# Two transformer blocks in one program: the opening's loads, transposes and table inputs put in another order

## The chip, the core and the metric

The kernel runs on one core of a Trainium2 chip: TensorE (PE), VectorE (DVE), ScalarE (ACT), GpSimd (POOL) and SyncE (SP), each with an instruction stream of its own, tied together by semaphores, and 16 DMA engines that move data between DRAM and the on-chip memory SBUF. TensorE writes into eight banks of PSUM. The metric is the device time of one execution in microseconds (us), the median over several; less is better.

## The reference

Two blocks over 256 tokens of 2048 features in float32. Only the head of the first block lies at the places of the change; in the first of its two layers it is, for x and for the context ctx alike:

```python
def first_block(x, c, ctx, c_ctx, ada_w, ada_b, norm_g, w_in, ...):
    for l in range(DEPTH):
        shift, scale, gate = jnp.split(jax.nn.silu(c) @ ada_w[l] + ada_b[l], 3, axis=-1)
        shift_c, scale_c, gate_c = jnp.split(jax.nn.silu(c_ctx) @ ada_w[l] + ada_b[l], 3, axis=-1)
        h = rmsnorm(x, norm_g[l]) * (1.0 + scale[:, None]) + shift[:, None]
        hc = rmsnorm(xc, norm_g[l]) * (1.0 + scale_c) + shift_c
        ...
        qc, kc, vc, upc, ufc, gc = split_proj(hc @ w_in[l])
        kc = rmsnorm(kc.reshape(B, C, N_KV_HEADS, HEAD_DIM), k_norm_g[l])
        q, k, v, up, uf, g = split_proj(h @ w_in[l])
        q = apply_axial_rope(rmsnorm(q..., q_norm_g[l]), cos, sin)
        k = apply_axial_rope(rmsnorm(k..., k_norm_g[l]), cos, sin)
        ...   # attention, pooling, Fourier mixing, gates, w_out, residual
    return rmsnorm(x, final_norm_g)
```

## The kernel before

**Chunks.** Every weight matrix is cut into chunks of 512 KB (`Chunk`), in a list `chunks` in the order in which TensorE multiplies them. A chunk of `ada_w` (an ada chunk) is multiplied as it is, by the silu of c and c_ctx: two float32 products in column groups of one bank (line 1221). A chunk of `w_in` and the others is split first: ScalarE rounds it to a high part (line 1463), VectorE subtracts that from it for a low part (line 1694), and TensorE does three fast products for each pair of tiles (lines 1240 to 1242: high x high, high x low, low x high), 24 products of 512 columns for a k/v chunk.

**Buffers.** SyncE loads the chunks in the order of the list `queue`, which before the change is equal to `chunks`, into `NRAW` = 8 buffers RAW. Load i waits until chunk i - 8 has been multiplied (an ada chunk; semaphore `chunk_multiplied`) or until its low part is made (any other; `split_lo`); SyncE issues in order, so one load that waits holds all behind it. The `NSPL` = 4 buffers SPL hold the split parts. `run_ahead` writes the split of a chunk into the engines' order `START_AHEAD` = 3 places ahead of the chunk that is being multiplied (from place 72 on 5).

**The order of the side work.** All engines take their instructions from one list `order`, into which `run_chunks` writes the products chunk by chunk, and between them tasks from the list `hi`. `pop_side(n)` takes n tasks from it. In the opening an ada chunk takes 2 tasks at every second chunk, a k/v chunk one for each half. So where a task stands in `hi` decides where it stands in the order of each engine, and an engine does what stands there strictly in order.

**The opening.** `start(u)` for u = 0 to 3 lays out two ada groups of 8 chunks, the scale (4 + u) and the shift (u) of features 512u to 512u + 511, and with u > 0 two k/v chunks among them; the last two follow. In places of `chunks`: ada 0 to 27, k/v at 28, 33, 46, 51, 64, 69, 70 and 71. Meanwhile:

- `square_x`, ScalarE: the squares of x and ctx.
- `turn_x(j)`, j = 0 to 15: TensorE turns 128 features of all tokens (line 1283), VectorE copies them out into XT (line 1705). Banks 0 to 2 take turns.
- `first_rstd`, after the 16 columns: `rstd_a` on VectorE and GpSimd (mean, power, four diagonals; lines 1711, 2102, 1716) and `rstd_b` on TensorE (line 1290), which spreads 1/rms over a bank.
- `tile_h(0, k, s)`: h of feature tile k for source s in three steps, VectorE, ScalarE, VectorE (lines 1738, 1481, 1743). Each needs the rms rows and the ada columns of its group, which come over `ada_out`, `ada_turn` (lines 1473, 1297, 1724).
- after the last shift group: `spill`, GpSimd's DMAs of XT to DRAM (4.19 MB, line 2097), since XT's place is used for the rows of q, k, v; `load_tables`, ScalarE's queue, three DMAs with the rope factors and the norm gains (lines 1490 to 1492), into one of the four TMP buffers; `tables`, VectorE (lines 1754, 1757); `load_dft`, GpSimd's queue, which waits for the second half of the copy.

`kv_out` follows the last k/v chunk: it flushes `hi`, then the k rows are copied out of banks 0 and 2 by ScalarE (line 1499) and of 1 and 3 by VectorE (line 1765), then the v columns of all four banks by ScalarE (line 1505). The first q chunk writes the same banks. From there on (`main0[1]`: q, pool, Fourier, gates) `mixed` puts two ada chunks, of the list `left`, behind every two others.

## Time and profile before

| | us |
|---|---|
| median of three runs | 2414.23 |
| lowest and highest | 2413.69, 2423.34 |
| the profiled execution | 2421.02 |
| its span, first to last instruction | 2419.2 |
| granted TensorE clock, mean | 0.984 |

The profile's page gives for each engine its busy time, for 40 equal slices (60.5 us each) the busy share in tenths, and the chain of work that ended last. A timeline row reads: start, length, engine, line, operation, output and input, how often, and in brackets the idle time before it and what ended it. "PEclk" is the granted share of TensorE's full clock of 2.4 GHz. A DMA share of 1.05 is what full engines show here.

### The profile page before, as it was taken

The page shows a single profiled execution, that of the slowest core. Times are in us where ns is not written, and L with a number is a line of the kernel's source. Part 1 is how long each engine was busy: PE and PEld are TensorE (multiplying, and loading weights), DVE is VectorE, ACT ScalarE, POOL GpSimd, SP SyncE. Part 2 cuts the span into 40 slices and gives each one's busy share as a digit, 9 for nine tenths or more (in the row PEclk, how much of TensorE's full clock was granted, in tenths as well). Part 3 has the DMA queues.
Part 4 walks back from the last instruction along what each step waited for, and adds up shares of the span by engine and source line. Part 5 has one row for each costly group of instructions (what it writes and reads, how often), then busy time and mean ns, then how long its engine had stood idle before and what let it go on. Part 6 is the DMA issues. An engine that isn't in the chain of part 4 may idle for free.

```text
span 2419.2 us, 30889 instructions
## 1 busy us (share of the span) xinstructions
PE 2316.2 (96%) x12239; PEld 1862.5 (77%) x12239; DVE 1313.2 (54%) x2114; ACT 1045.0 (43%) x1599; POOL 249.1 (10%) x325
## 2 busy tenths in 40 slices
PE   5889999999999979999999988999999999999998
PEld 2467777677777857678888867888888888888887
DVE  2444533132323254445777875667765777567764
ACT  2332333332322154445555654555544555355543
POOL 1000100000001121100011124111100110001111
PEclk9999999999999989999999998999999999999998
DMA  9864343335655456734566553566655555555552
GB/s 368 298 243 166 127 146 110 119 127 174 215 171 173 155 198 209 263 104 132 185 196 185 184 166 122 170 189 189 192 184 184 190 187 183 189 185 184 189 187 83
DMA packets 347023, 436.68 MB, mean 181 GB/s; under 512 B 13848, under 2 KB 269280, under 8 KB 345984
## 3 DMA queue, kind: packets, MB, share of 16 engines
q1 hardware_dynamic: 341376, 413.19, 51.6%
q0 software_dynamic: 3408, 16.38, 1.9%
q10 hardware_dynamic: 2096, 5.15, 0.6%
q8 instruction: 97, 1.59, 0.3%
q14 instruction: 46, 0.38, 0.0%
HBM read 428.37 MB, written 6.29 MB: 180 GB/s over the span
## 4 chain that ended last, share of the span: by engine, by line
PE 84%; DVE 6%; ACT 4%; DMA 3%; issue 2%; POOL 1%; SPq 0%; ACTq 0%; POOLq 0%; DVEq 0%
PE ps L1265 31%; PE ps L1266 16%; PE ps L1260 5%; PE ps L1262 5%; PE ps L1261 5%; PE ps L1240 4%; PE ps L1242 4%; PE ps L1241 4%; PE ps L1221 3%; DVE SPL L1694 2%; DMA RAW<-in_w_in_dram 2%; ACT SPL L1463 2%; PE ps L1312 1%; PE ps L1329 1%; PE ps L1355 1%
## 5 line engine op out<-in xcount | busy, mean ns | idle before, releaser
L1265 PE MATMUL ps<-HS,SPL 128*128 128x512 f32 x3456 | 1226.4, 400 | 5.9 <-POOL HS L2166 3.9
L1694 DVE TENSOR_TENSOR SPL<-RAW,SPL 128x1024 fp32r<-128x1024 f32 x592 | 750.5, 1271 | 634.2 <-ACT SPL L1463 631.7
L1266 PE MATMUL ps<-HS,SPL 128*128 128x256 f32 x3456 | 969.0, 280 | 0.0
L1463 ACT ACTIVATE SPL<-RAW 128x1024 fp32r<-128x1024 f32 x592 | 622.0, 1055 | 476.4 <-PE ps L1266 308.2
L1265 PEld LDWEIGHTS ps<-HS,SPL 128*128 128x128 f32 x3456 | 652.9, 189 | 166.4 <-POOL HS L2166 3.5
L1266 PEld LDWEIGHTS ps<-HS,SPL 128*128 128x128 f32 x3456 | 655.4, 190 | 2.0 <-issue 1.9
L1240 PE MATMUL ps<-SPL,HS 128*128 128x512 f32 x576 | 248.6, 432 | 27.2 <-ACT XT L1505 8.2
L1242 PE MATMUL ps<-SPL,HS 128*128 128x512 f32 x576 | 228.7, 397 | 0.0
L1241 PE MATMUL ps<-SPL,HS 128*128 128x512 f32 x576 | 228.3, 396 | 0.0
L1260 PE MATMUL ps<-HS,SPL 128*128 128x512 f32 x480 | 199.5, 416 | 1.2 <-DVE HS L1850 1.2
L1262 PE MATMUL ps<-HS,SPL 128*128 128x512 f32 x480 | 187.9, 391 | 0.0
L1261 PE MATMUL ps<-HS,SPL 128*128 128x512 f32 x480 | 187.8, 391 | 0.0
L1240 PEld LDWEIGHTS ps<-SPL,HS 128*128 128x128 f32 x576 | 110.8, 192 | 75.5 <-issue 18.5
L1241 PEld LDWEIGHTS ps<-SPL,HS 128*128 128x128 f32 x576 | 111.1, 193 | 26.9 <-issue 6.0
L1242 PEld LDWEIGHTS ps<-SPL,HS 128*128 128x128 f32 x576 | 110.3, 192 | 24.9
L2161 POOL TENSOR_TENSOR MM<-MM,GX 128x256 f32<-128x256 f32 x96 | 60.5, 650 | 653.7 <-DVE MM L1831 653.7
L1221 PE MATMUL ps<-RAW,CW 128*32 128x512 f32 x768 | 115.8, 637 | 9.7 <-DMA RAW<-in_ada_w_dram 7.8
L1260 PEld LDWEIGHTS ps<-HS,SPL 128*128 128x128 f32 x480 | 90.6, 189 | 41.0 <-issue 15.3
L1597 ACT ACTIVATE TMP<-XT 128x256 f32<-128x256 f32 (+1 forms) x74 | 33.9, 458 | 182.4 <-DVE XT L1862 113.7
L2154 POOL TENSOR_TENSOR TMP<-TMP 128x256 f32<-128x256 f32 (+1 forms) x67 | 60.7, 906 | 484.4 <-ACT TMP L1597 481.8
L1261 PEld LDWEIGHTS ps<-HS,SPL 128*128 128x128 f32 x480 | 90.5, 189 | 21.3 <-issue 3.8
L1262 PEld LDWEIGHTS ps<-HS,SPL 128*128 128x128 f32 x480 | 90.5, 189 | 19.7
(271 smaller groups left out, 1717.7 us busy)
## 6 DMA issues: line engine op xcount, KB each, us to landing
RAW<-in_w_in_dram SPq DMA_DIRECT2D x208, 512.0 KB, 5.7
RAW<-in_ada_w_dram SPq DMA_DIRECT2D x192, 512.0 KB, 4.8
RAW<-in_ffn_w_up_dram SPq DMA_DIRECT2D x192, 512.0 KB, 3.6
RAW<-in_w_out_dram SPq DMA_DIRECT2D x96, 512.0 KB, 4.5
RAW<-in_ffn_w_down_dram SPq DMA_DIRECT2D x96, 512.0 KB, 3.3
x_spill<-XT POOLq DMA_DIRECT2D x2, 2048.0 KB, 14.5
XT<-x_spill POOLq DMA_DIRECT2D x1, 4096.0 KB, 15.9
MM<-in_x_dram ACTq DMA_DIRECT2D x2, 1024.0 KB, 11.2
```

What stands on the lines that cost most here:

```text
L1221: m = mm(PS[6][32 * q:32 * q + 32, :], CW[:, 2 * k:2 * k + 32], raw_of(i)[:, kk * 512:(kk + 1) * 512], start=kc < 2, stop=kc >= 6, skip_gr ...
L1240: mm(PS[b][:, :], hr, wr, start=k == 0, stop=False, skip_group_check=True)
L1241: mm(PS[b][:, :], hr, wl, start=False, stop=False, skip_group_check=True)
L1242: m = mm(PS[b][:, :], hl, wr, start=False, stop=k == KT - 1, skip_group_check=True)
L1260: mm(PS[b][:, :], wr, hr, start=k == 0, stop=False, skip_group_check=True)
L1261: mm(PS[b][:, :], wr, hl, start=False, stop=False, skip_group_check=True)
L1262: m = mm(PS[b][:, :], wl, hr, start=False, stop=k == KT - 1, skip_group_check=True)
L1265: mm(PS[b][:, :], wr, hh, start=k == 0, stop=False, skip_group_check=True)
L1266: m = mm(PS[b][:, 256:512], wl, hh[:, 0:256], start=False, stop=k == KT - 1, skip_group_check=True)
L1463: act(SPL[:, (n - 1) % NSPL, 0, :], raw_of(i), ACT.Copy).then_inc(s_hi, 1)
L1694: tt(w[:, 1, :], raw_of(s["i"]), w[:, 0, :].bitcast(F32), ALU.subtract).then_inc(s_lo, 1)
L2154: tt(acc, acc, T(s["slot"])[:, 0:s["nt"] * 128], ALU.add).then_inc(s_accp, 1)
```

## The change

Eight edits, all at the opening:

- the k/v chunks stand after 8 of the 16 chunks of a `start` and at its end: places 24, 33, 42, 51, 60, 69, 70, 71
- `queue` is no longer `chunks`: each k/v chunk of the opening is loaded `KV_EARLY` = 3 places before its place of use. `c.load` is a chunk's place among the loads, `c.pos` among the products; the waits of both sides are written with the two
- in `start(0)` each ada chunk takes 2 tasks (side 3), so that two columns of x are turned per chunk; 12 idle tasks instead of 6 keep the first one where it was
- `first_rstd` becomes two tasks, after columns 1 and 3
- `spill` stands right behind the last column
- `tables_in` of the first layer as well, in a place of MM that holds x until it is turned, instead of in a TMP buffer; `tables` is put behind `load_dft`
- 4 ada chunks of `left` stand between the last k/v chunk and the first q chunk
- splits run 3 places ahead before place 71, 7 before place 76, 5 behind

```diff
         def load_ahead():
             while at["loaded"] < len(queue):
-                i = at["loaded"] - NRAW
                 last = []
-                if i >= 0 and queue[i].shape:
-                    if i >= at["taken"]:
+                if at["loaded"] >= NRAW:
+                    c = queue[at["loaded"] - NRAW]
+                    if c.pos >= (at["taken"] if c.shape else at["pos"]):
                         return
...
+                    last = [(s_lo, split_no[c.pos]) if c.shape else (s_chunk, c.pos + 1)]
...
-            while at["taken"] < min(len(queue), at["pos"] + (START_AHEAD if at["pos"] < 72 else at["ahead"])):
+            while at["taken"] < min(len(chunks), at["pos"] + (START_AHEAD if at["pos"] < 71 else 7 if at["pos"] < 76 else at["ahead"])):
...
-                    pop_side(2 if c.group.side == 2 and c.kc % 2 == 0 else 0)
+                    pop_side(2 if c.group.side == 3 or c.group.side == 2 and c.kc % 2 == 0 else 0)
...
-                x["tab"], last = take()
-                put("tables_in", l=l, slot=x["tab"], last=last + ([(s_colT, 3)] if both else x["ended"]))
+                if not both:
+                    x["tab"], last = take()
+                    put("tables_in", l=l, tab=T(x["tab"]), last=last + x["ended"])
...
-                cs = ada_group(0, 4 + u, 2) + ada_group(0, u, 2)
+                side = 2 if u else 3
+                cs = ada_group(0, 4 + u, side) + ada_group(0, u, side)
...
-                    if u == 3:
-                        put("spill", last=[multiplied()])
                     hi.extend(staged([tile_h(0, k, s, x, h) for k in range(4 * u, 4 * u + 4) for s in range(2)])
-                              + ([load_tables, tables, load_dft] if u == 3 else []))
+                              + ([load_tables, load_dft, tables] if u == 3 else []))
...
-                return cs[:12] + kv[2 * u - 2:2 * u - 1] + cs[12:] + kv[2 * u - 1:2 * u] if u else cs
+                return cs[:8] + kv[2 * u - 2:2 * u - 1] + cs[8:] + kv[2 * u - 1:2 * u] if u else cs
...
-        lay_out(main0[0] + mixed(main0[1], left))
+        n_start = len(main0[0])
+        head = main0[0] + left[:4]
+        del left[:4]
+        lay_out(head + mixed(main0[1], left))
...
+        for i in range(n_start):
+            if queue[i].shape:
+                queue.insert(i - KV_EARLY, queue.pop(i))
...
-        hi.extend([turn_x(j) for j in range(KT)] + [first_rstd])
+        turns = [turn_x(j) for j in range(KT)]
+        hi.extend(turns[:2] + [first_rstd_a] + turns[2:4] + [first_rstd_b] + turns[4:] + [lambda: put("spill", last=[]),
+                     lambda: put("tables_in", l=0, tab=MM[:, 7680:8192], last=[(s_turn, KT), (s_colT, 3)])])
```

What it moves, engine by engine. SyncE, the first loads; before:

```order
L1188 DMA RAW<-in_ada_w_dram 128x2x512 x8
L1188 DMA RAW<-in_ada_w_dram 128x2x512 [waits chunk_multiplied] x20
L1188 DMA RAW<-in_w_in_dram 128x2x512 [waits chunk_multiplied]
L1188 DMA RAW<-in_ada_w_dram 128x2x512 [waits chunk_multiplied] x4
L1188 DMA RAW<-in_w_in_dram 128x2x512 [waits chunk_multiplied]
L1188 DMA RAW<-in_ada_w_dram 128x2x512 [waits chunk_multiplied] x2
L1188 DMA RAW<-in_ada_w_dram 128x2x512 [waits split_lo]
L1188 DMA RAW<-in_ada_w_dram 128x2x512 [waits chunk_multiplied] x4
L1188 DMA RAW<-in_ada_w_dram 128x2x512 [waits split_lo]
```

and with the change:

```order
L1199 DMA RAW<-in_ada_w_dram 128x2x512 x8
L1199 DMA RAW<-in_ada_w_dram 128x2x512 [waits chunk_multiplied] x13
L1199 DMA RAW<-in_w_in_dram 128x2x512 [waits chunk_multiplied]
L1199 DMA RAW<-in_ada_w_dram 128x2x512 [waits chunk_multiplied] x7
L1199 DMA RAW<-in_ada_w_dram 128x2x512 [waits split_lo]
L1199 DMA RAW<-in_w_in_dram 128x2x512 [waits chunk_multiplied]
L1199 DMA RAW<-in_ada_w_dram 128x2x512 [waits chunk_multiplied] x7
L1199 DMA RAW<-in_ada_w_dram 128x2x512 [waits split_lo]
```

The first k/v load (`in_w_in`) goes from the 29th place to the 22nd, and the first load that waits for a split from the 37th to the 30th.

VectorE, from the second column of x on: before, the last columns, the first split and the rms chain (the columns before are left out; line 1694 is the split, 1705 the copy of a column, 1711 and 1716 the rms chain, 1738 the first step of h):

```order
L1694 TENSOR_TENSOR SPL<-RAW,SPL 128x1024 [waits split_hi]
L1705 COPY XT<-ps 128x2x256 [waits x_turned]
L1711 TENSOR_SCALAR SM<-SM 128x4 [waits x_squares]
L1716 TENSOR_SCALAR TMP<-IDN,SM 128x128 [waits rows_turned,rms_power]
L1716 TENSOR_SCALAR TMP<-IDN,SM 128x128 x3
L1738 SCALAR_TENSOR_TENSOR TMP<-XT,S,ps 128x256 [waits ada_turned,ada_scale,rstd_rows]
L1738 SCALAR_TENSOR_TENSOR TMP<-XT,S,ps 128x256 [waits ada_turned]
```

and with the change, the same work (lines 1705, 1716, 1722 and 1727, 1749):

```order
L1716 COPY XT<-ps 128x2x256 [waits x_turned] x2
L1722 TENSOR_SCALAR SM<-SM 128x4 [waits x_squares]
L1727 TENSOR_SCALAR TMP<-IDN,SM 128x128 [waits rms_power]
L1727 TENSOR_SCALAR TMP<-IDN,SM 128x128 x3
...
L1716 COPY XT<-ps 128x2x256 [waits x_turned] x14
L1735 TENSOR_REDUCE ADA<-ps 128x8 [waits ada_turned]
L1739 TENSOR_TENSOR ADA<-ADA,VV 128x8 [waits ada_summed]
L1749 SCALAR_TENSOR_TENSOR TMP<-XT,S,ps 128x256 [waits rows_turned,ada_scale,rstd_rows]
L1749 SCALAR_TENSOR_TENSOR TMP<-XT,S,ps 128x256 [waits ada_turned]
L1705 TENSOR_TENSOR SPL<-RAW,SPL 128x1024 [waits split_hi]
```

The rms chain stands between the second and the third column, all columns stand ahead of the first split.

TensorE, from the last k/v product to the first q product; before (1242 is the last k/v, 1240 the first q):

```order
L1240 MATMUL ps<-SPL,HS 128x512
L1241 MATMUL ps<-SPL,HS 128x512
L1242 MATMUL ps<-SPL,HS 128x512
L1240 MATMUL ps<-SPL,HS 128x512 [waits v_out,split_lo]
L1241 MATMUL ps<-SPL,HS 128x512
```

and with the change:

```order
L1252 MATMUL ps<-SPL,HS 128x512
L1253 MATMUL ps<-SPL,HS 128x512
L1232 MATMUL ps<-RAW,CW 32x512 [waits raw0_in,ada_out]
L1232 MATMUL ps<-RAW,CW 32x512
L1232 MATMUL ps<-RAW,CW 32x512 [waits raw1_in]
L1232 MATMUL ps<-RAW,CW 32x512
L1232 MATMUL ps<-RAW,CW 32x512 [waits raw2_in]
L1232 MATMUL ps<-RAW,CW 32x512
L1232 MATMUL ps<-RAW,CW 32x512 [waits raw3_in]
L1232 MATMUL ps<-RAW,CW 32x512
L1251 MATMUL ps<-SPL,HS 128x512 [waits v_out,split_lo]
L1252 MATMUL ps<-SPL,HS 128x512
```

Four ada chunks (line 1232) stand where TensorE went straight into the wait for the v copies.

## Rows read from the trace of the kernel before

**Rows 1.** The page, its parts 1 and 2: TensorE and the DMA engines over 40 slices
```profile
PE   5889999999999979999999988999999999999998
...
DMA  9864343335655456734566553566655555555552
```

**Rows 2.** Busy time by stretch: start:end, length, each engine, PEclk, DMA share, GB/s
```profile
0.00:4.00 4.00, 0.00 (x0) 0.00 (x0) 0.19 (x2) 0.00 (x0) 2.95 (x10) 1.00 0.48 119
...
4.00:60.00 56.00, 35.45 (x187) 13.33 (x187) 14.57 (x33) 12.37 (x14) 6.37 (x13) 0.99 1.05 386
...
60.00:84.00 24.00, 21.02 (x116) 12.59 (x116) 14.25 (x37) 8.92 (x17) 0.62 (x1) 0.89 0.58 203
...
100.00:112.00 12.00, 11.45 (x76) 6.13 (x68) 7.08 (x18) 4.56 (x10) 0.00 (x0) 1.00 0.88 304
...
134.00:148.00 14.00, 12.17 (x53) 9.43 (x52) 8.09 (x18) 4.80 (x9) 0.00 (x0) 1.00 1.01 413
...
156.70:161.00 4.30, 4.27 (x10) 3.43 (x11) 2.64 (x6) 2.27 (x4) 0.72 (x1) 0.50 0.07 27
...
161.00:200.00 39.00, 39.00 (x185) 29.38 (x185) 14.11 (x25) 8.28 (x12) 2.99 (x3) 1.00 0.38 131
```

**Rows 3.** Chain that ended last, 0 to 200 us: start, length in us, what
```profile
47.35 9.06 DMA RAW<-in_w_in_dram
...
61.67 2.06 PE ps L1290 x8
...
110.73 7.36 DMA RAW<-in_w_in_dram
...
157.92 0.43 PE ps L1242
...
165.09 0.24 PE ps L1242
```

**Rows 4.** Timeline while x is turned, and SyncE's next issue after the hole
```profile
36.52 1.09 PE L1283 MATMUL ps<-IDN,MM 128*128 128x128 f32 x8
...
37.21 1.29 DVE L1705 COPY XT<-ps 128x512 f32<-128x512 f32 x2 [0.73 <-PE ps L1283]
...
65.59 18.18 SPq L1188 DMA_DIRECT2D RAW<-in_ada_w_dram  x12
```

**Rows 5.** Waits of SyncE's queue, 0 to 200 us: total, times, longest
```profile
SPq L1188 <- DVE SPL L1694: 13.6, 7, 6.6
```

**Rows 6.** Timeline from the last k/v product to the first q product
```profile
148.88 0.66 ACT L1499 ACTIVATE XT<-ps 128x256 f32<-128x256 f32 x2 [6.19 <-PE ps L1242]
...
153.33 0.43 DVE L1754 TENSOR_TENSOR XT<-TMP,GX 128x256 f32<-128x256 f32 x1 [10.13 <-DMA GX<-in_k_norm_g_dram]
...
155.54 0.94 ACT L1505 ACTIVATE XT<-ps 128x256 f32<-128x256 f32 x3 [5.73 <-DVE XT L1765]
...
156.73 0.77 PE L1240 MATMUL ps<-SPL,HS 128*128 128x512 f32 x1 [7.89 <-ACT XT L1505]
```

**Rows 7.** DMA issues of the page: count, KB each, median us to landing
```profile
x_spill<-XT POOLq DMA_DIRECT2D x2, 2048.0 KB, 14.5
```

**Rows 8.** Timeline around the fifth to the eighth k/v chunk
```profile
120.47 0.80 PE L1240 MATMUL ps<-SPL,HS 128*128 128x512 f32 x1 [2.65 <-DVE SPL L1694]
...
127.51 1.92 PE L1221 MATMUL ps<-RAW,CW 128*32 128x512 f32 x16
...
130.06 1.18 POOL L2097 DMA_DIRECT2D x_spill<-XT  x2 [69.44 <-PE ps L1221]
...
133.17 1.22 DVE L1694 TENSOR_TENSOR SPL<-RAW,SPL 128x1024 fp32r<-128x1024 f32 x1
...
136.78 0.47 PE L1240 MATMUL ps<-SPL,HS 128*128 128x512 f32 x1 [1.18 <-DVE HS L1743]
...
148.40 0.75 POOL L2117 DMA_DIRECT2D XT<-in_k_dft_dram  x1 [17.16 <-DMA x_spill<-XT]
```

More of the change, by code:

```diff
@@ L20 @@
 AHEAD = 5
+KV_EARLY = 3
 START_AHEAD = 3
@@ L285, in run_ahead @@
                     last = [(s_chunk, chunk_split[at["split"] - NSPL] + 1)] if at["split"] > NSPL else []
-                    put("split", i=i, last=last)
+                    put("split", i=chunks[i].load, last=last)
                 at["taken"] += 1
@@ L1056, in two_block_program @@
         count["columns"] = 1
-        hi.extend([lambda: put("square_x")] + [idle] * 6 + [lambda: (columns([0, 1, 3, 4], False), columns([5, 6], True))])
+        hi.extend([lambda: put("square_x")] + [idle] * 12 + [lambda: (columns([0, 1, 3, 4], False), columns([5, 6], True))])
         def turn_x(j):
```

34 lines of the change are left out of this document (17 added, 17 removed).

## The prediction

> **What bounds the kernel now.** I read the page first. TensorE's line stands at nines almost throughout, but the first slices hold a five and an eight while the DMA engines stand at 9, 8, 6 there [rows 1]. So one stretch works by another limit. The busy time by stretch shows it: from 4 to 60 us the 16 DMA engines are full (share 1.05, 386 GB/s), from 60 to 84 us they fall to 0.58, from 100 to 112 to 0.88, and from 161 us on TensorE is full and the DMA engines idle more than half [rows 2]. Everything edited lies ahead of 161 us, so the question is how much earlier the same TensorE work of the first layer starts.
>
> Two holes stand there. The first is in the loads. The first k/v chunk is issued at 47.35 us and lands 9.06 us later; its split holds VectorE and ScalarE, behind which stands the last copy of x and the rms chain, and TensorE multiplies the rms rows only at 61.67 [rows 3]. TensorE consumes no weights meanwhile, no RAW buffer comes free, and SyncE issues no ada load until 65.59 [rows 4]. SyncE also waits 13.6 us in seven waits for the low half of a split [rows 5]. In engine time: 60 to 84 us lose (1.05 - 0.58) / 1.05 x 24 = 10.7 us, 100 to 112 lose (1.05 - 0.88) / 1.05 x 12 = 1.9, the shallow stretches between a further 0.2: 12.8 us lost before the fifth k/v chunk (the 65th load, chunk 64) lands at 110.73 + 7.36 = 118.1 [rows 2, 3]. As a control: 65 loads of 524 KB, 4.2 MB of x and ctx and some 0.6 of small inputs at 386 GB/s are 100.7 us; with 2.8 us lost in the first four (119 GB/s there [rows 2]) and the 12.8 they give 116.3, and it landed 1.8 later, the way from the last byte to the semaphore. The opening is bound by DMA traffic plus these holes.
>
> The second hole is at the end of k/v. ScalarE copies banks 0 and 2 at 148.88, but the rope tables wait for their inputs until 153.33, because VectorE has them ahead of its copies of banks 1 and 3; the v copies go at 155.54 and TensorE starts the q columns at 156.73, after 7.89 us idle [rows 6], which puts the end of k/v at 148.84.
>
> **The loads and the copy of x.** After the change the last ada chunk of the opening (chunk 68) is load 71, since the three last k/v chunks stand ahead of it. I go by landing times, from 118.1 us:
> - the 12.8 us of lost engine time go, as the k/v loads are there before their turn and the rms chain runs between turned columns long before the first k/v split: -12.8
> - the copy of x to DRAM, two DMAs of 2 MB [rows 7], ran from 130.06 with loads no one was yet waiting for, and now runs inside the full stretch. 4.19 MB at the 413 GB/s that 134 to 148 us show with both kinds mixed [rows 2] are 10.2 us: +10.2. Its lower bound is 0 (if it fell wholly into holes), its upper 18.3, from its issue at 130.06 until GpSimd's wait for it ends at 148.40 [rows 8]; I take the mixed rate, since no row shows a load stand still for it
> - the rope inputs, 0.39 MB in small pieces: +1.0 (0.5 to 2)
> - seven more loads before chunk 68, at 0.524 MB / 386 GB/s = 1.36: +9.5
> - turning x at twice the rate. Two turned columns take TensorE 1.09, and VectorE copies them in 1.29 [rows 4]; an ada chunk is a quarter of 1.92 [rows 8]. One chunk and two columns are so 1.6 us, longer than the 1.36 of a load; ten such places with the rms product and two ada turns let TensorE fall behind the loads from about chunk 10, by 2.3 us at chunk 15: +2.3 (0 to 6; below nothing it can't be, the loads are at full rate there now)
>
> Sum: 128.3, and with 0.5 to multiply the chunk 128.8, against 127.51 + 1.92 = 129.4 before [rows 8]. So the holes filled pay for the copy, and little more: -0.6 us. The Trainium skill (DMA: Bandwidth & Descriptors, section Issuing engines are not separate DMA queues) says that DMAs of all issuing engines run on the same 16 DMA engines and interleave. By that rule the copy is paid wherever the engines are full, as I take it; without it the result below would be 10.2 us better. The trace agrees: share 1.01 with both kinds in flight [rows 2].
>
> **The last three k/v chunks.** From chunk 68 to the last product were 148.84 - 129.4 = 19.4 us: three chunks of some 5.5, plus waits for h. One split of 1.22 us stood between the ada column and the scaled x on VectorE (133.17) [rows 8]; the order now has three splits ahead of the ada column and none behind: -1.2, which is just the 1.18 that TensorE waits there. Against it stands the clock: ahead of these three TensorE has five or six single ada chunks, each when its load lands. Before, the chunk after such a stretch began at 120.47 with products of 0.80, after a wait of 2.65 [rows 8], and lost some 1.8 us. The wait is gone now, since the split is early, so I take half: +0.9 (0 to 1.8). The Trainium skill (TensorE: Matmul & The Clock Gate, What's actually happening) holds that the slow clock is the default and activity lifts it; by it thin work too may bring the slow clock, which would be the 1.8. From 4 to 60 us such work stood at 0.99 [rows 2]; the trace decides neither.
>
> So k/v ends at 128.8 + 19.4 - 1.2 + 0.9 = 147.9, against 148.84: -0.9.
>
> **The end of k/v.** With tables made and the copy done, there remain the copies out of the banks: ScalarE two (0.66) and four v copies (0.94 for three), with TensorE starting 0.25 behind them [rows 6]: 2.2 us. TensorE does four ada chunks in it, 1.92 us [rows 8], taken from later in the layer, where TensorE is full. Before 7.89, now 2.2: -5.7, and -1.9 for the four chunks. The clock, 0.50 from 156.7 to 161 [rows 2], holds ten products at 0.43 instead of 0.24 [rows 3]: -1.9 with the gap gone. Their splits are made while k/v runs (the table of places ahead is 7 there), so they add nothing.
>
> **The rest.** The ada groups end four chunks earlier in the later stages; the same steps fall at other places. No row here shows what that moves; the nearest is the wait for h of 1.18 us [rows 8], so I put 0 with two such waits on either side, -2.4 to +2.4.
>
> Sum: -0.9 - 5.7 - 1.9 - 1.9 = -10.4 us. The profiled execution took 2421.0 (span 2419.2), 6.8 over the median of the three runs, 2414.2; the opening it shows belongs to either. So 2421.0 - 10.4 = 2410.6 for such an execution, and 2414.2 - 10.4 = 2403.8 for the median: 2404.
>
> **Rivals.**
> *The copy and the turning cost less.* If the copy starts at about 48 us, where the doubled turning leaves the loads thin, it uses just those 2.3 us; with the clock kept (-0.9), half the rope price, and the second layer gaining 1.5, it is -10.4 - 2.3 - 0.9 - 0.5 - 1.5 = -15.6: 2398.6. For it: loads and copy interleave. Against: by 48 us the thin stretch is nearly over.
> *The copy costs what it took.* The copy displaces loads for its 18.3 us, or the turning costs its upper 6 and the rope inputs and clock theirs (+5.6): +6 to +8, so about -3: 2411. For it: the DMA of x out and the weights lie in one set of engines, and it took 14.5 us a piece [rows 7]. The Trainium skill (DMA: Bandwidth & Descriptors, Queues, rings and completion order) says that an engine takes turns between queues packet by packet. By it loads may be thinned while the copy runs, and made up behind it: no change to the sum, only an idle TensorE then.
> *TensorE becomes the bound at the slow clock (the other side).* While the copy thins the loads, TensorE idles, and its clock falls. A k/v chunk at 0.43 a product takes 24 x 0.43 = 10.3 us, eight ada chunks at twice 0.48 take 7.7, with turns some 19.4 us, against 12.2 for nine loads. If the clock stayed low over four such rounds, each costs 7.2: +29, so +18.4: 2433. It decides only if 24 products in a row don't bring the clock back; before, they did within ten (156.7 to 161) [rows 2]. That speaks strongly against it.
> *The change doesn't do what it says.* If the rms chain still waited for a split, the hole at 54 to 65 would stay, with the copy on top: +12.8 - 10.4 = +2.4: 2416.6. The order of VectorE shows the chain ahead of every split, so hardly.
>
> **How the numbers follow.** Forecast -10.4: 0.52. Copy and turning cheap: 0.27. Copy at its full time: 0.13. No effect of the order: 0.04. Slow clock: 0.04. The 80% range reaches to the cheap case with the spread of the before runs (3 below) and to the dear one: 2395 to 2413. A measurement of this kernel can tell 0.5% from no change, 12.1 us. The forecast's own spread of about 4 us puts a third of it past 12.1 (0.17), and the cheap case nearly all (0.25): faster 0.42; slower by over 12.1 only the slow clock, 0.04; the rest, 0.54, within.
>
> **What the profile after would show.** Right: DMA share about 1.05 without a hole from 4 to 125 us but for a shallow dip near 40 to 50; the copy issued near 48; the last ada chunk near 129; k/v ending near 148; TensorE going on with ada chunks and the q columns 2 us behind, at clock 1.00. Wrong: a hole in the loads after 50 us (a split still stops SyncE), k/v chunks that start at half clock one after another, or the last k/v product after 152.

## The result, and the profile after

| | median us | range | runs |
|---|---|---|---|
| before | 2414.6 | 2413.7 to 2423.3 | 4 |
| after | 2442.2 | 2441.8 to 2445.3 | 4 |
| ratio after / before | 1.0105 | 95% interval 1.0081 to 1.0129 | |
| forecast | 2404 | 2395 to 2413 | |

The change makes the kernel slower by 1.05% in the ratio (the medians are 27.6 us apart), where a gain of 10 us was forecast; the worst rival stood at 2433. The profiled execution took 2442.5 (span 2440.7), so it is typical; that of before was 6.4 over the median of the four runs.

First the stretches of the opening, in the columns of [rows 2] (start:end, length, busy time of TensorE, its weight loads, VectorE, ScalarE and GpSimd, granted clock, DMA share, GB/s):

```profile
36.00:56.00 20.00, 19.30 (x124) 9.13 (x120) 11.53 (x22) 2.45 (x4) 1.18 (x2) 1.00 0.75 238
56.00:72.00 16.00, 3.78 (x8) 0.33 (x8) 2.76 (x7) 0.58 (x2) 0.00 (x0) 0.57 0.99 405
72.00:84.00 12.00, 11.32 (x52) 7.58 (x54) 5.00 (x12) 3.90 (x7) 0.00 (x0) 0.72 0.65 233
84.00:100.00 16.00, 13.55 (x76) 6.16 (x66) 7.50 (x18) 4.88 (x9) 0.00 (x0) 1.00 1.01 369
100.00:125.00 25.00, 22.89 (x119) 11.66 (x116) 9.12 (x23) 6.80 (x12) 0.00 (x0) 1.00 1.02 365
```

Where the engines moved 386 GB/s from 4 to 60 us before [rows 2], they now move 238 from 36 to 56, while TensorE is busy 19.3 of 20 us. The hole of 60 to 84 us is not gone but has moved to 72 to 84, and the shallow 100 to 112 is filled. TensorE's timeline (start, length, line, operands, count, idle time before and what ended it) shows both causes:

```profile
42.29 1.05 PE L1232 MATMUL ps<-RAW,CW 128*32 128x512 f32 x4
43.27 1.09 PE L1294 MATMUL ps<-IDN,MM 128*128 128x128 f32 x8
44.30 1.05 PE L1232 MATMUL ps<-RAW,CW 128*32 128x512 f32 x4
...
51.30 0.66 PE L1294 MATMUL ps<-IDN,MM 128*128 128x128 f32 x4
...
58.21 1.86 PE L1232 MATMUL ps<-RAW,CW 128*32 128x512 f32 x4 [2.72 <-DMA RAW<-in_ada_w_dram]
69.96 1.92 PE L1232 MATMUL ps<-RAW,CW 128*32 128x512 f32 x4 [9.89 <-DMA RAW<-in_ada_w_dram]
...
73.41 0.78 PE L1251 MATMUL ps<-SPL,HS 128*128 128x512 f32 x1
```

A place with one ada chunk and two turned columns takes 2.0 us, from 42.29 to 44.30. The last column is turned at 51.3, and GpSimd issues the copy of x at 52.98. After that TensorE gets no ada chunk between 58.2 and 70.0: it idles 9.89 us, and starts the first k/v chunk at half clock (0.78 for the first product).

The last ada chunk of the opening ends at 142.0 (forecast 128.8), the last k/v product at 161.0 (forecast 147.9). The end of k/v is then as forecast, and right behind it comes something that wasn't:

```profile
161.00 1.93 PE L1232 MATMUL ps<-RAW,CW 128*32 128x512 f32 x16
...
172.51 0.66 PE L1315 MATMUL ps<-IDN,XT 128*128 128x128 f32 x2 [3.66 <-DVE XT L1806]
172.82 0.78 PE L1251 MATMUL ps<-SPL,HS 128*128 128x512 f32 x1
173.39 0.63 PE L1252 MATMUL ps<-SPL,HS 128*128 128x512 f32 x1
```

The four ada chunks take 1.93, the first q product starts at 163.12, 2.1 us behind k/v and at full clock (granted clock 1.00 from 161 to 165 us, where it was 0.50 before [rows 2]). But TensorE then waits 3.66 us for a norm that it has to turn (the k rows, normed by VectorE; L1315 is L1304 of before) and loses the clock: its products have a length of 0.63 instead of 0.39. What VectorE waited for itself stands in the rows of ScalarE, SyncE and VectorE:

```profile
162.09 0.88 SPq L1199 DMA_DIRECT2D RAW<-in_w_in_dram  x2
...
165.59 1.06 ACT L1474 ACTIVATE SPL<-RAW 128x1024 fp32r<-128x1024 f32 x1 [2.72 <-DMA RAW<-in_w_in_dram]
...
166.68 2.56 DVE L1705 TENSOR_TENSOR SPL<-RAW,SPL 128x1024 fp32r<-128x1024 f32 x2 [4.82 <-ACT SPL L1474]
```

Two q loads, the ninth and the tenth from the first early ada chunk on, take the buffers of the first early chunks and are issued only at 162.09, when these have been multiplied. Their splits stand ahead of the norm on ScalarE and VectorE, so the norm waits for two loads.

The largest part lies further on. The waits of TensorE from 165 to 1100 us, of before first and of after below it (line, what it waited for: total, times, longest):

```profile
PE ps L1240 <- POOL HS L2111: 5.5, 4, 3.6
PE ps L1304 <- DVE MM L1795: 4.5, 2, 3.8
...
PE ps L1240 <- ACT MM L1499: 2.9, 1, 2.9
PE ps L1297 <- ACT TMP L1473: 2.6, 3, 1.0
...
PE ps L1304 <- DVE XT L1798: 0.8, 2, 0.4
```

```profile
PE ps L1315 <- DVE MM L1806: 12.5, 3, 6.5
PE ps L1315 <- DVE XT L1806: 10.0, 5, 3.7
PE ps L1308 <- ACT TMP L1484: 6.8, 3, 3.9
PE ps L1251 <- POOL HS L2122: 4.0, 4, 1.4
```

TensorE waited 5.3 us for the norms of q and its neighbours (L1304) in this stretch, and now 22.5 (L1315, the same line); for the ada column (L1297, now L1308) 2.6 and now 6.8.

### The profile page after: what moved, and what is told of

The parts are those of the page before. It is cut to its first block, busy times and chain, and to the rows that moved or that the text cites. A ratio compares the mean times of both kernels' runs of the same rounds, so it can differ in the third digit from the quotient of the medians.

```text
span 2440.7 us, 30874 instructions
## 1 busy us (share of the span) xinstructions
PE 2319.6 (95%) x12239; PEld 1858.3 (76%) x12239; DVE 1315.7 (54%) x2114; ACT 1044.1 (43%) x1599; POOL 250.4 (10%) x325
## 4 chain that ended last, share of the span: by engine, by line
PE 84%; DVE 6%; ACT 4%; DMA 3%; issue 2%; POOL 1%; SPq 0%; ACTq 0%; POOLq 0%; DVEq 0%
PE ps L1276 31%; PE ps L1277 15%; PE ps L1271 5%; PE ps L1273 4%; PE ps L1272 4%; PE ps L1251 4%; PE ps L1253 4%; PE ps L1252 4%; PE ps L1232 3%; DMA RAW<-in_ada_w_dram 2%; DVE SPL L1705 2%; ACT SPL L1474 2%; PE ps L1323 1%; PE ps L1340 1%; PE ps L1366 1%
## 5 line engine op out<-in xcount | busy, mean ns | idle before, releaser
L1232 PE MATMUL ps<-RAW,CW 128*32 128x512 f32 x768 | 123.3, 631 | 29.8 <-DMA RAW<-in_ada_w_dram 27.9
L1271 PEld LDWEIGHTS ps<-HS,SPL 128*128 128x128 f32 x480 | 90.1, 188 | 42.6 <-issue 16.1
```

The source lines that it names most:

```text
L1232: m = mm(PS[6][32 * q:32 * q + 32, :], CW[:, 2 * k:2 * k + 32], raw_of(c.load)[:, kk * 512:(kk + 1) * 512], start=kc < 2, stop=kc >= 6, sk ...
L1271: mm(PS[b][:, :], wr, hr, start=k == 0, stop=False, skip_group_check=True)
```

## The experiments

Each kernel's ratio is to the kernel before on the same chip, with its 95% interval. "First q product" is where the opening ends in the profiled execution (156.73 before; before_delay4, which has the code of the kernel before up to there, shows 160.09, so a single profile of the opening is good for some 3 us). "Growth" is how much later the same products of TensorE run than in the kernel before at 1040 to 1080 us, less what it was at 160 to 200 us: the n-th start of each line of code (ada products left out) is compared in both traces, and the median of the differences taken. Kernels that leave the order behind the opening as it was (before_copy_early, before_rms_early) show -2.0 and -3.2, so a growth within some 3 us of nothing is none. A growth without a subtraction is the difference alone.

| kernel | ratio | interval | first q product | growth, us |
|---|---|---|---|---|
| after | 1.0105 | 1.0081 to 1.0129 | 163.12 | 27.1 - 10.6 = 16.5 |
| copy_late | 1.0108 | 1.0089 to 1.0128 | 161.96 | 26.4 - 7.3 = 19.1 |
| turn_old | 1.0086 | 1.0066 to 1.0105 | 152.16 | 16.2 - 0.1 = 16.1 |
| no_head | 1.0012 | 0.9999 to 1.0026 | 160.76 | -0.7 - 2.7 = -3.4 |
| before_head | 1.0099 | 1.0073 to 1.0124 | 163.21 | 24.6 - 7.0 = 17.6 |
| head_phase | 1.0008 | 0.9994 to 1.0023 | 161.46 | 0.5 - 3.5 = -3.0 |
| before_delay4 | 1.0086 | 1.0059 to 1.0112 | 160.09 | 19.2 - 3.7 = 15.5 |
| before_head8 | 1.0025 | 1.0007 to 1.0043 | 162.17 | 6.3 - 5.9 = 0.4 |
| nh_turn_old | 0.9953 | 0.9935 to 0.9970 | 153.46 | -7.3 + 3.8 = -3.5 |
| nh_to_copy_late | 0.9956 | 0.9936 to 0.9975 | 149.07 | -2.7 |
| copy_halves | 0.9959 | 0.9947 to 0.9971 | 149.34 | -3.1 |
| kv_late | 1.0005 | 0.9993 to 1.0018 | 163.44 | -3.5 |
| turn_pairs | 1.0007 | 0.9992 to 1.0022 | 162.22 | 0.2 |
| copy_at_kv0 | 1.0008 | 0.9992 to 1.0023 | 164.02 | -0.5 |
| pairs_halves | 0.9970 | 0.9951 to 0.9989 | 153.83 | -0.7 |
| before_copy_early | 0.9993 | 0.9974 to 1.0011 | 156.94 | -2.0 |
| before_rms_early | 0.9993 | 0.9978 to 1.0008 | 159.03 | -3.2 |

### The four early ada chunks: taken out, and alone

```diff
 (after)
-        head = main0[0] + left[:4]
-        del left[:4]
+        head = main0[0]
-... (START_AHEAD if at["pos"] < 71 else 7 if at["pos"] < 76 else at["ahead"])
+... (START_AHEAD if at["pos"] < 72 else at["ahead"])
```

> The changed kernel without the four ada chunks between the k/v and the q columns (they go back to their places later in the layer), and with the k/v table of places ahead (3, then 5) of the kernel before. The opening up to the last k/v product stays as in the changed kernel. Theory A (the later losses come from these four chunks: the two q loads that wait for them, the seven splits made ahead that stand in front of the k norm chain, and every later ada group at another place): the wait of 3.66 us of TensorE for the turned norms and the half clock from 172 us go, and the offset to the kernel before stays at some 11 to 13 us from 170 us to the end instead of growing to 27 and ending at 22. Time 2442 - 7 = 2435. Theory B (the four chunks fill a gap of 2 us and the later growth has another cause): 2442 + 2 = 2444, with the same growth after 250 us.

Measured: 1.0012. The growth is gone (-3.4), and so is the wait of 3.66 us. Its size had been expected at 7 us; it was some 22 (2442.2 to 2420.0 in the medians, 0.9% in the ratios). Theory A holds with three times its price. The edit also takes back the table of seven places, so the chunks alone are the next run.

```diff
 (before)
-        lay_out(main0[0] + mixed(main0[1], left))
+        head = main0[0] + left[:4]
+        del left[:4]
+        lay_out(head + mixed(main0[1], left))
```

> The kernel before with one part of the change alone: four ada chunks of later groups stand between the k/v columns and the q columns. The number of places looked ahead stays at its old values. They fall into the 7.89 us in which TensorE waits for the v copies, so they are free there and give back 1.9 us later. Theory A (moving the ada groups costs in the rest of the layers): 2414 - 2 + 8 = 2420, and the offset against the kernel before grows in the stretch 200 to 1050 us. Theory B (the move is neutral there): 2412.

Measured: 1.0099, nearly the whole loss of the change from four chunks in another place. Its trace has a pair of waits for turned norms near 223 and 229 us (the change has the same 0.90 and 2.26 at 226.54 and 232.18), again near 287 and 293, and larger ones in the second layer, where the kernel before has 3.79 us and none:

```profile
163.21 0.76 PE L1242 MATMUL ps<-SPL,HS 128*128 128x512 f32 x1 [10.13 <-DVE SPL L1696]
222.95 0.63 PE L1306 MATMUL ps<-IDN,XT 128*128 128x128 f32 x4 [0.93 <-DVE XT L1797]
228.59 0.63 PE L1306 MATMUL ps<-IDN,XT 128*128 128x128 f32 x4 [2.26 <-DVE XT L1797]
...
918.55 1.09 PE L1306 MATMUL ps<-IDN,MM 128*128 128x128 f32 x4 [4.50 <-DVE MM L1797]
925.70 1.09 PE L1306 MATMUL ps<-IDN,MM 128*128 128x128 f32 x4 [6.07 <-DVE MM L1797]
```

The first row is another cost, of this kernel alone. Most of its 10.13 us is the wait for the v copies that the kernel before has too (the last ends at 160.87 here). Behind them ScalarE and VectorE make the first q split, since that chunk now stands four places later and wasn't within the places looked ahead while k/v ran: 2.3 us more. The change's table of seven places took that part away (0.20 there).

What differs at 222.95 is seen against the same group in the kernel before:

```profile
208.70 0.47 PE L1240 MATMUL ps<-SPL,HS 128*128 128x512 f32 x1 [0.59 <-DVE XT L1765]
...
211.55 0.60 PE L1297 MATMUL ps<-IDN,TMP 128*128 128x128 f32 x4
...
215.75 0.69 DVE L1795 TENSOR_TENSOR XT<-TMP 128x512 f32<-128x512 f32 x1
...
217.48 0.60 PE L1304 MATMUL ps<-IDN,XT 128*128 128x128 f32 x4
```

The group starts at 208.70, an ada column is turned at 211.55 (12 products in), and the first norm at 217.48 (36 products in), 1.0 us after VectorE has finished it (215.75 + 0.69). With the four chunks elsewhere the group starts at 216.32 and no ada column is due. The steps beside the products stand in one list and are given out one per half chunk, so the norm's turn moves forward by the step that the ada column held: to 222.95, 24 products in. VectorE's chain ends at 222.11 + 0.69, too late: TensorE waits 0.93 for it, and 2.26 for the second norm. The order was traced at this one group; that the larger waits of the second layer come in the same way rests on the next three runs.

### Phase, or chunks done early?

By phase is meant where an ada group of eight chunks ends against the weights group into which it is mixed: at its end, as in the kernel before, or in its middle.

```diff
 (after: the first four places inside the first q group stay bare)
-        lay_out(head + mixed(main0[1], left))
+        lay_out(head + main0[1][:4] + mixed(main0[1][4:], left))
```

> The changed kernel with the four early ada chunks kept between the k/v and the q columns, but taken from the first four places inside the first q group, which then has its first four chunks bare. From the sixth q chunk on every ada chunk stands where it stood in the kernel before. Theory A (phase: an ada group that ends in the middle of a weights group no longer puts its column and turn between the end of a group and the first turned norm, so the norm chain of VectorE comes too late; 0.9 and 2.3 us at each such place): the waits of TensorE for turned norms of 0.9 and 2.3 us near 225 and 290 us, and of 4.5 and 6.5 near 920 go, the offset to the kernel before stays flat from 190 us on. Time 2442 - 16 = 2426. Theory B (any four chunks moved cost in this way, wherever from, by the splits and loads they shift): 2442. The wait of 3.66 us at 172 us and the half clock behind it may stay by both, since the two q loads still wait for the four.

Measured: 1.0008, with the four chunks as early as in the change. Growth -3.0. TensorE's waits from 165 to 1100 us in it:

```profile
PE ps L1251 <- POOL HS L2122: 5.8, 3, 3.5
PE ps L1315 <- DVE MM L1806: 4.2, 2, 3.8
...
PE ps L1315 <- DVE XT L1809: 1.1, 3, 0.4
PE ps L1315 <- DVE XT L1806: 1.1, 2, 0.6
```

The norms are back at 6.4 us. The wait near 172 us, which both theories let stand, went too (0.61 at 167.79). That is no sign against the two q loads: with the four places bare, the third and fourth q chunks are loads 78 and 79, which SyncE had issued by 145.1 and which landed by 151.7, and the splits ahead of the norm are theirs. In the change they were loads 80 and 81, issued at 162.09 and landed at 165.56 and 166.90. So this edit takes away two costs, the wait for two loads and the moved end of the later ada groups; the offset at 160 to 200 us (10.6 and 3.5) has the first, with 1.7 that the opening itself ended earlier, the growth (16.5 and -3.0) the second.

```diff
 (before: the same four places bare, nothing early)
-        lay_out(main0[0] + mixed(main0[1], left))
+        lay_out(main0[0] + main0[1][:4] + mixed(main0[1][4:], left))
```

> The kernel before with one thing changed: the first four places inside the first q group stay bare of ada chunks, so that every ada group from the ninth on ends four chunks LATER than before; none is done early. Theory A (it is the phase, an ada group ending in the middle of a weights group instead of at its end, and not that chunks were taken ahead): the same waits as with four taken ahead, 0.9 and 2.3 us for the turned norms near 215 to 290, some 10 near 920, and 16 to 20 us in all: 2416 + 16 = 2432. Theory B (loads and splits are shifted by the chunks taken ahead): 2416.

Measured: 1.0086, growth 15.5, with waits of 0.92 and 2.26 at 218.47 and 224.11. Four chunks later cost as four chunks earlier.

```diff
 (before)
-        lay_out(main0[0] + mixed(main0[1], left))
+        head = main0[0] + left[:8]
+        del left[:8]
+        lay_out(head + mixed(main0[1], left))
```

> The kernel before with eight ada chunks (one whole group) between the k/v and the q columns, taken from later. Theory A (phase): every later group ends where one ended before, so from 200 us on the offset stays flat; the q columns start later, since their loads wait for the eight (about 10 us idle as with four, and 3.8 us of work that is given back later): 2416 + 5 = 2421. Theory B (each chunk taken ahead costs): more than the 24 us that four cost, 2440 or above.

Measured: 1.0025, growth 0.4. Eight early cost a quarter of what four do, and only in the opening. The three runs agree that the growth hangs on whether an ada group ends where it ended before, at the end of a weights group.

### The opening: turning x, and the copy

```diff
 (after)
-                side = 2 if u else 3
+                side = 2
-... [idle] * 12 ...
+... [idle] * 6 ...
```

> The changed kernel with x turned at the old rate: two columns at every second ada chunk, and six empty steps instead of twelve ahead of them; all else stays. Theory A (a lone ada chunk between turned columns takes TensorE as long as two do, so the doubled turning let TensorE and with it the loads fall behind): the DMA share from 36 to 56 us comes back from 0.75 to about 1.0, some 4 to 6 us of engine time, but the copy of x is issued some 8 us later and starves the loads there just the same. Time 2442 - 4 = 2438, with the end of the opening (last ada chunk) near 138. Theory B (the doubled turning costs the 2.3 us that the forecast gave it): 2440. Theory C: the later copy meets the first k/v chunks and the time rises by 3 to 5.

Measured: 1.0086 against 1.0105, 4.6 us, with intervals that overlap; the offset to the kernel before at 160 us falls from 10.6 to 0.1, more than the time shows. The share from 36 to 56 us is 1.05, as theory A said, and the one from 72 to 84 us 0.98 instead of 0.65.

> The changed kernel without the four early ada chunks and with x turned at the old rate; the early loads of the k/v weights, the early rope inputs, the early copy of x and the early rms chain stay. If the two costs are apart and add up (the four chunks 22 us, the turning 6 to 10 us in the opening), it stands 7 to 10 us under the kernel without the four chunks: 2418 - 6 = 2412, ratio 0.9975, with the last k/v product near 150. If the doubled turning only cost because of the four chunks: 2420.

This kernel has that edit and the one of no_head. Measured: 0.9953, faster than the kernel before by 0.3 to 0.65%, where 0.9975 was expected. Its stretches:

```profile
36.00:56.00 20.00, 16.69 (x118) 8.51 (x116) 11.93 (x25) 2.25 (x3) 0.60 (x1) 1.00 1.05 387
56.00:72.00 16.00, 11.57 (x48) 7.03 (x48) 7.70 (x17) 4.91 (x9) 1.18 (x2) 0.79 1.03 404
72.00:84.00 12.00, 11.15 (x60) 5.92 (x60) 4.48 (x12) 3.88 (x7) 0.00 (x0) 1.00 1.02 362
```

No hole is left up to 125 us. With the turning of the change, everything else equal, it is 1.0012 (no_head): the first q product stands 7.3 us later (160.76 against 153.46), and the ratios differ by 0.6%, 14 us; the trace bears out some 7.

```diff
 (after, behind the last turned column; and in start 3)
-                     [..., lambda: put("spill", last=[]), ...]
+                    if u == 3:
+                        put("spill", last=[multiplied()])
```

> The changed kernel with one thing put back: the copy of x to DRAM is issued at the end of the fourth start (about 130 us) as in the kernel before, no longer behind the last turned column. Theory A (the copy starves the loads): it is what makes TensorE wait 2.72 and 9.89 us for ada loads between 58 and 70 us and run at half clock until 80. Without it the 16 loads land about 10 us earlier, the first k/v chunk runs at full clock, and the last ada chunk of the opening ends near 130 instead of 142; the late copy then makes the rope tables or the v copies wait a little. Time about 2442 - 9 = 2433. Theory B (bytes only count, wherever they move): the last ada chunk comes 10 us earlier as well, but the copy then delays the last k/v chunks and q by as much, so the time stays within 3 us of 2442. Theory C: TensorE's slow turning is what costs, and the time stays at 2442 because the loads are late anyway.

Measured: 1.0108, the same as after. The last ada chunk of the opening ends 8.5 us earlier (133.6), but TensorE then waits 5.28 us for scaled x at 152.52: nearer to theory B.

> As the one before it in this set, and the copy of x at its old place (about 130 us) as well. If the copy starves the loads wherever they are needed at once, the early place costs 10 us of engine time at 57 to 72 us and the late one delays the last three k/v chunks and the tables by some 5: 3 to 5 us less than with the early copy, 2408. If the engines are full from 4 to 140 us in either case and the copy costs its bytes at both places: the same, 2412. If the late copy holds the tables and the scaled x: 2415.

> The kernel with x turned at the old rate and without the four early ada chunks, with the first 2 MB of the copy of x issued behind the last turned column, and the other 2 MB at the end of the fourth start (about 127 us). If the copy costs its bytes wherever the engines are full, and only the part that falls into the thin stretch of 56 to 72 us (share 0.53 where the copy is late, 1.03 where it is early) is free: the best of the three, 2403. If it is all the same: 2406, as with either place of the whole copy.

Measured: 0.9956 and 0.9959. The whole copy early (0.9953), late, or half and half are the same within the intervals. Where it is late, the hole in the loads is back:

```profile
56.00:72.00 16.00, 11.40 (x56) 6.38 (x56) 8.52 (x19) 4.91 (x9) 0.00 (x0) 0.89 0.53 180
...
59.20 0.76 PE L1252 MATMUL ps<-SPL,HS 128*128 128x512 f32 x1 [3.50 <-DVE HS L1755]
```

So the early k/v loads and the early rms chain, which this kernel has, don't remove it: TensorE waits 3.50 us for scaled x and then multiplies the first k/v chunk, no buffer comes free, and the engines stand at 0.27 from 60 to 64 us and at 0.00 from 64 to 68. That is (1.05 - 0.53) / 1.05 x 16 = 7.9 us of engine time, and in nh_turn_old it is the copy that fills it. The profiled first q product is 4.4 us earlier with the late copy (149.07), which the times don't confirm. That the half-and-half version would be best isn't shown.

```diff
 (before: the copy alone)
-                    if u == 3:
-                        put("spill", last=[multiplied()])
-        hi.extend([turn_x(j) for j in range(KT)] + [first_rstd])
+        hi.extend([turn_x(j) for j in range(KT)] + [lambda: put("spill", last=[]), first_rstd])
```

> The kernel before with one part alone: the copy of x to DRAM issued right behind the last turned column (about 54 us) instead of at 130 us. Theory A (it starves the ada loads behind it by 10 to 12 us): part of that falls into the hole that stands there anyway (TensorE waits 7.64 us for the rms chain and the loads stand still until 65.59), so the loads come some 6 us later, and the gain at the end (scaled x and tables no longer wait for the copy) is 3 at most: 2418 + 3 = 2421. Theory B (the copy fits the hole between 56 and 72 us, with a DMA share of 0.63): 2418 - 5 = 2413.

Measured: 0.9993, no difference, though the copy fills the stretch from 56 to 72 us (share 1.03, before 0.63): neither theory's price.

```diff
 (no_head, copy at the seventh ada chunk of start 1, ahead of the first k/v chunk)
+                if u == 1:
+                    cs[6].then = lambda: put("spill", last=[multiplied()])
```

> The changed kernel without the four early ada chunks, x turned at twice the rate as in the change, and the copy of x put eight ada chunks later, just ahead of the first k/v chunk. Theory A (what the early copy costs hangs on what TensorE has in hand while the copy takes the engines: eight ada chunks that each need a load, as in the change, and it idles 10 us; or a k/v chunk of 6 us whose load and split are there): TensorE's idle 9.9 to 10.6 us shrinks to 3 or less, and the time is 2407, as with the old turning. Theory B (the doubled turning itself costs 7 us, since TensorE falls behind the loads at 36 to 50 us): 2415 to 2418, as the kernel without the four chunks.

Measured: 1.0008. TensorE's idle time behind the copy did shrink, to 3.68 us at most (10.57 in no_head), as theory A said, and the time did not move: theory B. The long idle stretch looks dear, but its length doesn't set the time, since the DMA engines are full in it.

```profile
36.00:56.00 20.00, 19.22 (x124) 9.02 (x120) 12.00 (x23) 2.85 (x5) 0.00 (x0) 1.00 0.78 245
56.00:72.00 16.00, 10.78 (x40) 5.79 (x40) 6.07 (x16) 2.91 (x6) 1.18 (x2) 0.79 0.93 361
72.00:84.00 12.00, 7.33 (x26) 1.14 (x28) 1.23 (x1) 1.06 (x1) 0.00 (x0) 0.86 1.02 391
```

Against the three rows of nh_turn_old above, (387 - 245) x 20 = 2.8 MB were not moved in the first and (404 - 361) x 16 = 0.7 MB in the second: 9.1 us at 387 GB/s. The first q product stands 10.6 later.

```diff
 (no_head: four columns behind two ada chunks)
-... pop_side(2 if c.group.side == 3 or c.group.side == 2 and c.kc % 2 == 0 else 0)
+... pop_side((4 if c.group.side == 3 else 2 if c.group.side == 2 else 0) if c.kc % 2 == 0 else 0)
```

> The changed kernel without the four early ada chunks, and with the same doubled turning given out in fours: two ada chunks, then four turned columns, where the change puts two columns behind each chunk. Theory A (a lone ada chunk between turned columns takes TensorE 1.0 us, as much as two in a row): four columns and two chunks take 2.2 + 1.0 = 3.2 us for two loads (2.7 us) instead of 4.0, so most of the shallow stretch at 36 to 56 us goes; from 2420 down by 3 to 5: 2416. Theory B (the columns themselves, their banks and their copies out are what takes the time): four columns in a row wait for VectorE, no gain, 2420 or above. The early copy starves the loads in either case.

Measured: 1.0007 against 1.0012. Two chunks and four columns do take 3.0 us instead of 4.0 (42.31 to 45.33 in its timeline), but no time came back, and 36 to 56 us moved 303 GB/s against the 295 of no_head. The kernels with the change's turning show 238 (after), 245 (copy_at_kv0), 251 (head_phase) and 295 there, so this window alone doesn't tell. Theory A fell as a remedy, and that the lone chunk is the whole of the turning's cost is not shown.

> As the one before it, with the doubled turning given out in fours behind two ada chunks, and only half of the copy ahead of the first k/v chunk, the other half at the end of the fourth start. A candidate: if theory A of the run before holds, the turned columns are done 2 us sooner than in the change and no load is starved for long: 2404, as the best so far (0.9959 of the kernel before). If the doubled turning costs by itself: 2412.

Its edits are those of the last two, with one half of the copy there and the other in start 3. Measured: 0.9970, between; not better than the old turning.

### The early loads and the early rms chain

```diff
 (nh_turn_old)
-KV_EARLY = 3
+KV_EARLY = 0
```

> The kernel with x turned at the old rate and without the four early ada chunks (0.9953 of the kernel before), with the k/v weights loaded in their own places instead of three places ahead. Theory A (the hole at 54 to 65 us came from a k/v split for which the rms chain and the last copy of x waited; both the early loads and the early rms chain are needed): each k/v chunk waits some 2.6 us for its split again, as in the kernel before at 94 and 120 us, 5 to 8 us lost, 2407 + 5 = 2412. Theory B (the early rms chain alone fills the hole, and the loads are bound by bytes, so their order means nothing): 2407.

Measured: 1.0005 against 0.9953, 12 us. Five of the eight k/v chunks wait for their split, 3.60 to 5.55 us, where it was 2.65 before [rows 8]; three of them:

```profile
91.75 0.79 PE L1250 MATMUL ps<-SPL,HS 128*128 128x512 f32 x1 [3.60 <-DVE SPL L1704]
107.97 0.79 PE L1250 MATMUL ps<-SPL,HS 128*128 128x512 f32 x1 [3.79 <-DVE SPL L1704]
123.09 0.80 PE L1250 MATMUL ps<-SPL,HS 128*128 128x512 f32 x1 [3.87 <-DVE SPL L1704]
```

```diff
 (before: the rms chain alone; first_rstd split in two as in the change)
-        hi.extend([turn_x(j) for j in range(KT)] + [first_rstd])
+        hi.extend(turns[:2] + [first_rstd_a] + turns[2:4] + [first_rstd_b] + turns[4:])
```

> The kernel before with one part alone: the rms chain of x goes between the turned columns (its first half behind the second column, its second behind the fourth) instead of behind the last. Theory A (the chain stood behind a split for which it waited): TensorE multiplies the rms rows near 45 us instead of 61.67, VectorE's wait falls away, the DMA share from 60 to 84 us rises from 0.58 to 0.8 or more, and the time falls by 4 to 8: 2418 - 6 = 2412. Theory B (the split itself, waiting for its 9 us landing, is the hole, whatever stands behind it): 2418.

Measured: 0.9993, no difference; the share from 56 to 72 us is 0.61 (before 0.63), and the first k/v chunk waits 6.19 us for scaled x. The time is that of theory B. That the landing of the split's chunk is the hole doesn't follow: with early loads and a late copy the hole is there too (nh_to_copy_late).

## Why the prediction was wrong, and where it was right

**"The rest": the step that failed most.** The forecast put 0 with 2.4 us on either side for the ada groups that end four chunks earlier. The place alone costs 1.0105 - 1.0008 = 0.97%, 23 us. In the traces the changed kernel and head_phase are 7.1 us apart at 160 to 200 us (3.66 of waiting and eleven products at 0.43 a step instead of 0.23 are 5.9 of it), 26.6 at 1040 and 21.6 in the span. So some 6 us are the wait for the two q loads and the clock lost by it, and the rest is the phase. The first part belongs to another sentence of the forecast, that the splits made ahead "add nothing": it held for the first two q chunks (0.20 us of waiting), not for the next two, whose loads needed the buffers of the early chunks. The forecast took one wait for h as the nearest row and asked what four chunks move by themselves. The number that decided was in the code: an ada group has eight chunks, so moving four shifts its end from the end of a weights group to its middle, at every later group and in both layers, and takes from the list of side steps the one that gave VectorE the length of 12 products for the norm. With waits of up to 6.5 us at place after place, a bound from one wait was no bound. The order of steps on TensorE and the length of the norm chain would have shown it, and both were at hand.

**Turning x: the term was mis-sized.** Forecast +2.3 (0 to 6). Measured by bytes in after: (387 - 238) / 387 x 20 = 7.7 us; in no_head, with the same code there, (387 - 295) / 387 x 20 = 4.8. The step that failed is "one chunk and two columns are so 1.6 us": the chunk was put at a quarter of 1.92, and a lone one between turned columns takes 1.0 (42.29 to 43.27), as much as two did. (Two chunks of a pair write different column groups of the bank, by `q = 2 * (kc % 2) + kk` in the code; whether that is why a pair takes no longer than one was not tested.) A place is 2.0 against the load's 1.36. Taken out, it gives 0.6% with the four chunks gone and 0.2% with them, 5 to 14 us; the first q products say 7.3 and 11.0. That the lone chunk is all of it was argued and is not borne out (turn_pairs).

**The copy of x.** Forecast +10.2 at a mixed rate, with the fear of 18.3. Its place makes no difference that can be measured (0.9953, 0.9956, 0.9959). The reason given for the mixed rate, that no row shows a load stand still, was wrong: in after they nearly do. By DMA queue, from 58 to 62 us and from 62 to 66 us (q0 carries the copy, q1 the loads: packets, MB, share of 16 engines):

```profile
q0 software_dynamic: 94, 1.54, 90.1%
q1 hardware_dynamic: 66, 0.14, 8.7%
...
q0 software_dynamic: 107, 1.49, 87.1%
q1 hardware_dynamic: 108, 0.22, 14.2%
```

A packet of the copy is 1.54 / 94 = 16.4 KB in the first stretch (in the second, 16 of only 4 bytes lower the mean to 13.9), one of the loads 2.0. Over both stretches the queues have about as many packets, 201 and 174, so the loads get 0.36 MB where the copy gets 3.03, less than an eighth of it. The Trainium skill (DMA: Bandwidth & Descriptors, Queues, rings and completion order) says that an engine drains one packet from a queue and then goes to the next. The counts fit that roughly, but not stretch by stretch (94 against 66, 107 against 108), and that the packets of this profile are those of the page is not shown. The prediction cited that rule and drew from it a thinning that is made up behind, "only an idle TensorE then". copy_at_kv0 fits this: with the idle time cut to a third, the time stayed.

**The slow clock.** The rival at 2433 needed four rounds at the low clock. There was one: 56 to 72 us at 0.57 and 72 to 84 at 0.72, then 1.00. While the first k/v chunk runs at half clock the loads fill all buffers, and then they stop:

```profile
76.00:80.00 4.00, 4.00 (x13) 3.18 (x12) 2.75 (x5) 2.08 (x3) 0.00 (x0) 0.65 0.83 303
80.00:84.00 4.00, 4.00 (x32) 1.93 (x32) 0.11 (x1) 0.00 (x0) 0.00 (x0) 1.00 0.09 7
```

From 72 to 84 us that is (386 - 233) / 386 x 12 = 4.8 us of engine time: right in kind, one round of 7.2 where four were feared.

**The hole in the loads.** The forecast had 12.8 us of lost engine time go "as the k/v loads are there before their turn" and the rms chain runs early. nh_turn_old has no hole from 4 to 125 us, but this reason is right only in part: nh_to_copy_late has both and still loses 7.9 us from 56 to 72. In nh_turn_old the copy lies in that stretch, so some 7.9 of the -12.8 and of the +10.2 are one and the same bytes' time; the two errors cancel in the sum. The early loads are worth their 12 us (kv_late), the early rms chain alone nothing that was measured.

**What held.** The last three k/v chunks took 18.9 us (forecast 19.1, before 19.4). The four ada chunks took 1.93 (forecast 1.92), and the first q product came 2.1 us behind k/v (forecast 2.2) and at full clock. Without the turning term and the moved chunks the sum would have been -10.4 - 2.3 + 1.9 = -10.8 us; nh_turn_old, which is the change without these two parts, measured -0.47%, 11 us (7 to 16). So the rest of the sum agrees as a sum, in part by luck: two of its terms cancel (above), and the trace has the first q product only 3.3 us earlier than in the kernel before (6.6 against before_delay4).

**The sum of the miss.** 2442 - 2404 = 38 us: 23 for the place of the four chunks (some 6 the two q loads, the rest the phase), the 1.9 that the early chunks were to give (head_phase has them and is no faster than no_head), and 3 to 12 of turning beyond its 2.3. That leaves 1 to 10 us that no run divides.

## What to carry to other kernels

Where side work is given out by counting main steps, moving some of it shifts everything behind it: before pricing such a move, take its length modulo the group, and look at the first two groups behind it for a chain that ends less than one step ahead of its use. If four must go early, leave four places bare behind them (head_phase), so that the later ends stay where they were. Look also at which loads need the buffers of what was moved, and what stands behind their splits. And price a stretch bound by DMA in bytes moved: shortening TensorE's idle time under full DMA engines brought nothing (copy_at_kv0), while a busy TensorE that lets the loads fall to 238 of 387 GB/s loses two fifths of the stretch in bytes. Before counting a hole in the loads as gone, ask what will move bytes in it.

## What the runs showed of the hardware that was not expected

A lone ada chunk of four 128x512 products between turned columns took 0.98 to 1.05 us at full clock, two in a row 1.06 (in the kernel before, 207.05). Where the queue of the copy with packets of 16.4 KB and that of the loads with 2.0 KB both had work, from 58 to 66 us, they moved 201 and 174 packets, so the loads got 0.36 MB and the copy 3.03: a load of 524 KB issued at 62 to 66 us took 18.0 us to land. The openings of equal programs differ by some 3 us from one execution to the next (the first q product at 156.73 and 160.09 with the same code ahead of it), so a single profile doesn't settle a term of 2 us there.
